# Latent attention written out over 64 query blocks, with projections by half tiles between them

## What is computed

```python
q = jnp.einsum("bsr,re->bse", rmsnorm(c_q, q_norm_g[l]), w_q_up[l])
q = q.reshape(b, s, MLA_HEADS, MLA_QK_DIM)            # 64 plain + 32 rotated
q_nope, q_rope = q[..., :MLA_NOPE_DIM], q[..., MLA_NOPE_DIM:]
q_rope = apply_rope(q_rope, cos, sin)
kv = jnp.einsum("bsr,re->bse", rmsnorm(c_kv, kv_norm_g[l]), w_kv_up[l])
k_nope, v_mla = kv[..., :MLA_NOPE_DIM], kv[..., MLA_NOPE_DIM:]
k_full = jnp.concatenate([k_nope, broadcast(apply_rope(k_rope, cos, sin))], -1)
o_mla = chunk_causal_softmax_attention(q_full, k_full, v_mla)
```

## Time and profile before

| | |
|---|---|
| median of 3 runs | 3533.0 us (3526.06 to 3537.19) |
| profiled execution | 3531.41 us, of which the span of its instructions 3529.6 us |
| `latent_attention` in it | first matmul at 688.16 us, last VectorE instruction starts at 1067.61 us |
| busy over the span | PE 3006.8 (85%), DVE 1612.5 (46%), ACT 1256.4 (36%), POOL 711.3 (20%) |

### The profile page before, as it was taken

How to read it: one execution, slowest core, us unless ns; L and a number is a source line. 1 busy time by engine, 2 the same in 40 slices (tenths; PEclk the granted TensorE clock), 3 DMA queues, 4 the chain that set the end, 5 groups by cost and what they waited for, 6 DMA issues and landing times. The chain is left out here.

```text
span 3529.6 us, 35907 instructions
## 1 busy us (share of the span) xinstructions
PE 3006.8 (85%) x13416; PEld 2422.7 (69%) x13416; DVE 1612.5 (46%) x1983; ACT 1256.4 (36%) x2003; POOL 711.3 (20%) x317
## 2 busy tenths in 40 slices
PE   6999998766668859989889899977686998998998
PEld 5787886555556747767767677754475787787786
DVE  3665651356654333777877787511432221111121
ACT  3555541344442143555555445432223111111110
POOL 2111111100002211323332233211312121121211
PEclk8999999888869979999999999988798999999999
DMA  4111222000004312121221112133230111111112
GB/s 111 38 54 48 66 67 59 18 8 7 9 0 146 111 66 63 48 61 38 62 60 50 55 51 75 69 137 107 95 125 18 48 48 42 42 48 42 42 48 72
DMA packets 232494, 207.77 MB, mean 59 GB/s; under 512 B 25224, under 2 KB 196776, under 8 KB 232360
## 3 DMA queue, kind: packets, MB, share of 16 engines
q1 hardware_dynamic: 231328, 204.40, 18.6%
q10 hardware_dynamic: 1032, 1.57, 0.3%
HBM read 156.13 MB, written 41.42 MB: 56 GB/s over the span
## 5 line engine op out<-in xcount | busy, mean ns | idle before, releaser
L179 POOL TENSOR_TENSOR w_lo<-w_raw,w_hi 128x1024 fp32r<-128x1024 f32 (+2 forms) x228 | 536.5, 2355 | 2214.7 <-ACT w_hi L171 2214.7
L171 ACT ACTIVATE w_hi<-w_raw 128x1024 fp32r<-128x1024 f32 (+2 forms) x228 | 223.7, 985 | 780.1 <-PE u_y_ps L1649 222.4
L2272 DVE SCALAR_TENSOR_TENSOR d_acc<-d_padded,vectors,d_acc 128x1024 f32<-128x1024 f32 x240 | 397.2, 1655 | 4.5
L197 PE MATMUL d_pp<-h_hi,w_hi 128*128 128x512 f32 x896 | 368.0, 411 | 12.2 <-PEq L67 5.2
L197 PE MATMUL d_pp<-h_hi,w_lo 128*128 128x512 f32 x896 | 368.8, 412 | 0.0
L197 PE MATMUL d_pp<-h_lo,w_hi 128*128 128x512 f32 x896 | 366.0, 408 | 0.0
L197 PE MATMUL s_pp<-h_hi,w_hi 128*128 128x512 f32 x512 | 206.8, 404 | 12.1 <-PEq L67 12.1
L197 PEld LDWEIGHTS d_pp<-h_hi,w_hi 128*128 128x128 f32 x896 | 175.1, 195 | 56.0 <-issue 18.0
L2056 POOL TENSOR_TENSOR d_probs<-d_probs 128x128 f32<-128x128 f32 (+3 forms) x64 | 123.5, 1930 | 410.4 <-ACT d_probs L2170 410.2
L197 PE MATMUL s_pp<-h_hi,w_lo 128*128 128x512 f32 x512 | 205.2, 401 | 0.0
L197 PE MATMUL s_pp<-h_lo,w_hi 128*128 128x512 f32 x512 | 204.2, 399 | 0.0
(11 more groups left out here) (320 smaller groups left out, 6621.0 us busy)
## 6 DMA issues: line engine op xcount, KB each, us to landing
w_raw<-in_w_in SPq DMA_DIRECT2D x97, 512.0 KB, 4.0
w_raw<-in_w_gate_up SPq DMA_DIRECT2D x44, 512.0 KB, 3.9
w_raw<-in_w_down SPq DMA_DIRECT2D x22, 512.0 KB, 3.8
gates<-s_gate SPq DMA_DIRECT2D x16, 512.0 KB, 5.2
f_gate<-gates SPq DMA_DIRECT2D x16, 512.0 KB, 4.8
w_raw<-in_w_out SPq DMA_DIRECT2D x16, 512.0 KB, 4.1
w_raw<-in_w_proj SPq DMA_DIRECT2D x16, 512.0 KB, 5.0
x_tok_in<-in_x SPq DMA_DIRECT2D x8, 512.0 KB, 8.5
```

The source lines that it names most:

```text
L171: act.activation(self.hi[:, s, 0:chunks, :], self.raw[:, s, 0:chunks, :], ACT.Copy).then_inc(self.rounded[s], 1)
L179: pool.tensor_tensor(self.lo[:, s, 0:chunks, :], self.raw[:, s, 0:chunks, :], f32(self.hi[:, s, 0:chunks, :]), ALU.subtract).then_inc(self ...
L197: mm = pe.matmul(halves(ps)[h], w[:, k, :], x[:, k, h * HALF:(h + 1) * HALF], start=(k == 0 and r == 0), stop=(k == chunks - 1 and r == 2))
L2272: dve.scalar_tensor_tensor(out=acc[:, :], in0=x, scalar=wt, in1=acc[:, :], op0=ALU.mult, op1=ALU.add).then_inc(c["taps"], 1)
```

## The change

`latent_attention` is written anew, in the form of one sequence of 64 units (8 heads by 8 blocks) plus 4 steps that empty it, with no loop and no `convert` between pairs:

- **Projections.** There are 16 tiles in a list: `X` and `Y` (the rotated parts of four heads at a time, plain and with halves swapped), `N` (the 64 plain query rows of two heads), `K`, `V`. The first five are made before step 0, by halves of 512 tokens in the four halves of the score buffers. The others are made in 22 halves of 6 or 9 matmuls at the steps of the table `when`, each between the scores and the turning of that step, into one bank `pp`. ScalarE rounds a half straight from PSUM and VectorE subtracts straight from PSUM (`take`, `split`); `m_raw` is gone.
- **Copies.** Queries and keys are put in place by DMA, SBUF to SBUF: six transfers per head (two of 128 KB, four of 256 KB), on SP's queue between the weight loads.
- **Banks.** Both chunks of turned probabilities go into `bank[n % 2]`, never into the score buffers. The value tile is turned at step 6 of each head, for the next head, through the same two banks in two halves (64 turnings in all, before 32).
- **Turned probabilities** have two buffers `t_hi`, `t_lo`, and the values are multiplied four steps behind (before three), after the turning of that step.
- **VectorE order.** In a step, the norm of unit `s-1` stands ahead of the maximum of unit `s`. The maximum is negated in the same instruction; the scale is in the queries, so L1159 is gone. The gate is applied in 16 pieces of 64x512.
- `latents` loads the rotation table as two tiles of 128 rows, in 8 transfers instead of 1, and keeps its inverse roots in a part of the gate tile that is not written yet.
- The weights of the next stage are rounded at step 46.

```diff
-    PAIRS, UNITS, ROWS = SB_W // P, 2 * QB, 64
-    TILES = 4
+    UNITS, LAG = HEADS_ * QB, 4
+    STEPS = UNITS + LAG
...
+        when = {5: (-1, 1), 6: (2, 3), 7: (8, 9), 8: (18, 19), 9: (20, 21), 10: (22, 23), 11: (24, 25), 12: (26, 27),
+                13: (33, 34), 14: (36, 37), 15: (41, 42)}
...
+            def copy(head):
+                a, p = head % 2, head // 2
+                r = slice(head % 4 * ROPE, (head % 4 + 1) * ROPE)
+                if head >= 2:
+                    sp.wait_ge(c["scored"], QB * (head - 1))
+                sp.wait_ge(c["r_low"], head // 4 + 1)
+                for dst, src in ((q_hi, r_hi), (q_lo, r_lo)):
+                    sp.dma_start(f32(dst[NOPE:QK, a, :]), src[r, :].bitcast(F32)).then_inc(copied[a], 16)
...
+            after = {6: (0, 1), 9: (2, 3), 12: (4,), 13: (5,)}
@@ ScalarE @@
+            for s in range(STEPS):
+                head, at = s // QB + 1, s % QB
+                if s < UNITS:
+                    expose(s)
+                for t, h in halves_at(s):
+                    take(t, h)
+                if at == CONV_V and head < HEADS_:
+                    for x in range(2):
+                        round_v(head, x)
+                if 2 <= s < UNITS + 2:
+                    for x in range(CHUNKS[(s - 2) % QB]):
+                        round_t(s - 2, x)
+                if s >= LAG and (s - LAG) % 2 == 1:
+                    copy_low((s - LAG) // 2)
@@ VectorE @@
+            for s in range(STEPS):
+                head, at = s // QB + 1, s % QB
+                if 1 <= s <= UNITS:
+                    norm(s - 1)
+                if s < UNITS:
+                    top(s)
+                for t, h in halves_at(s):
+                    split(t, h)
...
+                if 2 <= s < UNITS + 2:
+                    for x in range(CHUNKS[(s - 2) % QB]):
+                        low_t(s - 2, x)
+                if s >= LAG and (s - LAG) % 2 == 1:
+                    add_low((s - LAG) // 2)
@@ TensorE @@
+            for s in range(STEPS):
+                head, at = s // QB + 1, s % QB
+                if s < UNITS:
+                    score(s)
+                for t, h in halves_at(s):
+                    fill(t, h)
+                if at == CONV_V and head < HEADS_:
+                    for x in range(2):
+                        turn_v(head, x)
+                if 2 <= s < UNITS + 2:
+                    for x in range(CHUNKS[(s - 2) % QB]):
+                        turn_t(s - 2, x)
+                if s >= LAG and (s - LAG) % 2 == 1:
+                    values(s - LAG)
```

More of the change, by code:

```diff
@@ L818, in latents @@
         square = mem.sb("l_square", [P, 2, TOK])
[L819 removed]
+        inv = [gate_silu[:, n, :] for n in (2, 3)]
         turn = square
@@ L975, in latent_attention @@
-        pp = mem.ps("m_pp")
+        o_sb = mem.sb("m_o_sb", [P, HALF])
+        pp = mem.ps("m_pp", [P, HALF])
         sc = [mem.ps(f"m_sc{i}") for i in range(2)]
[L977 to L985, removed]
@@ L1000, in latent_attention @@
[L1000 to L1004, removed]
-        complete = [next(u for u in range(UNITS) if runs[u][1] >= ENDS[j]) for j in range(TILES)]
-        first_chunk = [sum(CHUNKS[x % QB] for x in range(u)) for u in range(UNITS + 1)]
-        rows = [slice(0, ROWS), slice(ROWS, P)]
-        EACH = 2 * N_CHUNKS
-        def turned_into(u, c):
-            return sc[(u + 1) % 2][:, HALF:TOK] if c else bank
@@ L1014, in latent_attention @@
-        ring.phase(PAIRS, 3, 3, 2, 2, ahead=ahead)
+        bank = [mem.ps(f"m_bank{i}", [P, HALF]) for i in range(2)]
+        o_ps = mem.ps("m_o_ps", [P, 2 * P])
+        names = """n_round n_low k_round k_low taken_v turned_x turned_y r_sum r_round r_low scored masked maxed prob inverse
+            normed turned t_round t_low pv o_copied o_done gate_mul""".split()
+        c = {n: mem.sem(f"m_{n}") for n in names}
+        copied = [mem.sem(f"m_copied{i}") for i in range(2)]
+        COPIES = 6
@@ new lines, in latent_attention, with halves_at, bank_of @@
+        round_at = {7: 2, 8: 5, 9: 11, 10: 20, 11: 22, 12: 24, 13: 29, 14: 34, 15: 38}
+        AHEAD_AT = 46
+        def halves_at(s):
+            return [(t, h) for t in when for h in range(2) if when[t][h] == s]
+        banks = [half for x in sc for half in halves(x)]
+        def bank_of(t, h):
+            return banks[(2 * t + h) % 4] if t < EARLY else pp[:, :]
+        first = [N_CHUNKS * (u // QB) + sum(CHUNKS[:u % QB]) for u in range(UNITS + 1)]
+        CONV_V = 6
+        order = [("v", 0, 0), ("v", 0, 1)]
@@ L1015, in latent_attention @@
+        ring.phase(1, *(len(source(t)) for t in range(TILES)), ahead=ahead)
         block = stack.enter_context(nc.Block())
@@ new lines, in fill, with turn_v @@
+            def fill(t, h):
+                own(t, 3 * chunks[t] * h, 3 * chunks[t] * (h + 1))
+            def turn_v(head, x):
+                n = number["v", head, x]
+                pe.wait_ge(c["taken_v"], 2 * (head // 2 + 1))
+                if n >= 2:
+                    pe.wait_ge(c["t_low"], n - 1)
+                for b in range(4):
+                    t = pe.transpose(bank[n % 2][:, b * P:(b + 1) * P], v_raw[:, (4 * x + b) * P:(4 * x + b + 1) * P],
+                                     ident[:, :])
+                t.then_inc(c["turned"], 1)
@@ new lines, in values @@
+            def values(u):
+                g, (head, b) = u // 2, divmod(u, QB)
+                pe.wait_ge(c["t_low"], number["t", u, CHUNKS[b] - 1] + 1)
+                if g >= 1:
+                    pe.wait_ge(c["o_done"], g)
+                for k in range(b + 1):
+                    q0 = P if k == b else 0
+                    for x, t in enumerate((t_hi, t_lo)):
+                        mm = pe.matmul(o_ps[:, q0:2 * P], v2[:, k, head % 2].rearrange("p x d -> p (x d)"),
+                                       t[:, g % 2, k, q0:2 * P], start=(k == 0 and x == 0), stop=(k == b and x == 1))
+                mm.then_inc(c["pv"], 1)
```

537 lines of the change are left out of this document (276 added, 261 removed).

## The result

The changed kernel runs in 3484.0 us (median of 4 runs, 3477.4 to 3488.6) against 3535.1 of the kernel before (4 runs, 3526.1 to 3537.7): a ratio of 0.9859, with an interval of 0.9834 to 0.9883. The forecast was 3488 and 45 us less; 51 us less were measured. The profiled execution took 3477.4 us, its span is 3475.5.

The account below looks back on a forecast made before the run. No engine is full; a chain of hand-offs bounds the stage. First mask 717 plus 254 + 10 + 10.5 + 15.5 + 11 + 8 gives 1026, 45 us less: 3488 us, eight in ten from 3460 to 3515.

Parts of the forecast that it names:

- Step 7: Beginning of the stage, with five tiles and the copies for heads 0 and 1: first mask at 717, maybe 713 or 723.
- Step 1 and 2: Chain of eight heads at 31.8 us, 254 us, plus the gate's 16 multiplications on VectorE's path, 10 us.
- Step 3: Values' turning, seven times in the loop, with value halves first in both banks: 1.5 us each, 10.5 us.
- Step 4 and 5: Half tiles in the loop: ScalarE's and VectorE's work on them 15.5 us, TensorE late at them 11 us.
- 6, end: Steps 64 to 67, which empty the sequence: 8 us, then 0.85 us to the next stage.
- the 10 us a head: Kernel before, steps with two chunks: TensorE late by a taken score buffer or value matmuls ahead; expected to go.
- filled against unfilled pair: Kernel before: 91 us against 74, less 8 for `convert`, is 9 per pair or 27 for three.
- rival C: Slower: TensorE at 1.2 GHz throughout, decides if the mean clock falls below 0.52; 3551 us, chance 0.03.
- B: TensorE still ends the steps with many half tiles: 32 us more than A, 3520 us, chance 0.16.
- A: The forecast: the chain as summed, TensorE's lateness at half tiles between 0 and 25; 3470 to 3505 us, chance 0.60.
- The hidden case: Additions, gate and takes fall into unseen waits, up to 30 of 47 us go; 3458 us, chance 0.15.
- D: No change: the old waits return in another place, for instance score buffers; 3525 to 3540 us, chance 0.06.

Follow-up runs that it names:

- experiment 1: Changed kernel with VectorE's norm of unit s-1 behind the maximum of unit s: 3444.4 us, ratio 0.9746.
- Experiment 5: Changed kernel with the next head's value halves turned one each at steps 4 and 5, not both at step 6: 3467.0 us, ratio 0.9816.
- experiment 4: Changed kernel with only the first and last matmul of each half tile in the loop, so not the reference's values: 3477.9 us (1 run).
- experiment 3: Changed kernel with the half tiles of steps -1 and 1 at steps 2 and 3, the next two at 4 and 5: 3476.2 us (1 run).
- experiment 12: Changed kernel with values three steps behind, one buffer of turned probabilities, second piece in the score buffer, values ahead of the turning: 3524.2 us, ratio 0.9973.
- 11: Changed kernel with values three steps behind, one buffer of turned probabilities, and values ahead of the turning on TensorE: 3498.2 us, ratio 0.9896.
- experiment 10: Changed kernel with norm behind the maximum, value halves at steps 4 and 5, first half tiles at steps 2 to 5: 3428.9 us, ratio 0.9710.
- experiments 6 and 7: Each against the changed kernel. First: values three steps behind, one buffer of turned probabilities, 3515.4 us. Second: second piece in the score buffer, 3508.7 us.
- experiment 9: Changed kernel with values three steps behind, one buffer of turned probabilities, and the second piece in the score buffer: 3543.5 us, ratio 1.0036.
- the ladder: Kernels from the one before to the changed one, stages 383.9, 385.4, 356.1, 342.2, 340.5 us; the first step is a bundle, the others one edit each.

## Why the prediction was right, and where it only came out

The mechanism was right, the direction and the size too: 3484 against 3488, 43.4 us of stage against 45, and 306.4 us from the first mask to the next stage's first transfer where the text named 310. But the sum is better than its terms, and that it came within 2 us of the stage is luck: three terms missed by +5, +14 and -17 us and cancelled.

| step of the prediction | predicted, us | measured, us |
|---|---|---|
| 7, first matmul to first mask | 28.8 | 34.1 |
| 1 and 2, eight heads with the gate | 264 | 8 x 32.8 = 262 |
| 3, seven turnings of values | 10.5 | 7 x 3.5 = 24.5 |
| 4 and 5, half tiles | 26.5 | 9 |
| 6, end (measured: what is left) | 8.85 | 10.5 |
| stage | 339 | 340.5 |

The last line before the sum takes up what the others leave: the first head, which has no low parts or values to work on at first and holds the half tiles of steps 1 to 3, is counted like a full head without tiles.

*Step 1 and 2 held to one per cent,* and piece by piece. The last head has neither turning nor half tile and takes 32.8 us; the prediction had 31.8 + 1.3. In it VectorE is busy for 21.0 us (the prediction's terms for VectorE sum to 21.9) and idles 10.4 us under exponentials and roundings (predicted 10.0 and 1.1 for hand-offs). Only 1.1 us of its waits go back to TensorE (0.5 for scores, 0.6 for the copy of o), so the 10 us a head are gone as forecast. That the norm goes on the path was forecast and priced at 4.16 + 1.2, and experiment 1 took 4.6 us a head off by moving it. What I did not ask is whether the change needs it there. It doesn't: norm(s - 1) waits for the exponentials of the step before, and nothing in the new order of banks and buffers hangs on its standing first.

*Step 3 was mis-sized,* and beyond its upper bound of 2.5. Head 7, with a turning and no half tile, takes 36.3 us against 32.8 for the last. I had rounding 0.4, low part 0.42 and turning 0.6 plus hand-offs, as if one half were in the way. The row shows 2.10: VectorE's low parts follow the pair of roundings, the first four turnings of the probabilities take 1.1 us from issue to ScalarE's start, and both wait their turn. The scores behind it add 0.51. The last 0.9 of the 3.5 lies in other steps of the head (0.25 from block 7 to 0, 0.66 from block 1 to 2), and no run tells what it is. Experiment 5 shows the cause from the other side.

*Step 4 and 5 were too high by 17.* Heads 2 to 6, which hold 18 of the half tiles, take 36.7, 39.3, 40.9, 37.1 and 36.0 us against 36.3 with a turning alone: 9 in sum. TensorE's lateness, put at 11, is about 4 (experiment 4, at its lower clock). The waits of ScalarE and VectorE for `m_pp` in the loop sum to 3.6 us where I named 11. The comparison by which I sized them, filled against unfilled pair, had the old kernel's collisions of scores and low parts in it, and these are not a property of the tiles. It also priced 0.65 a half for ScalarE; 9 - 4 = 5 us over 18 halves is 0.3. Most of a rounding falls where ScalarE would wait anyway.

*Step 7 was 5.3 short,* though inside its bounds of 713 to 723, counted from the first matmul too (24.8 to 34.8; the stage began 3 us earlier). The prediction named the right wait, of ScalarE's half tile of step -1 for both heads' copies, and sized it too low: issuing the twelve takes from 702.42 to 713.66, 11.2 us and not about 6, and the last lands 5.3 us after its issue began and not 3 to 4. It also took the wait as given, where VectorE's order makes it one: experiment 3 moves the half tile and has 6.0 us back.

*The clock.* Granted was 0.80 over the stage (0.79 before), and the sum did not need it, but for the 2 us that it moved at the stage's end. The experiments bear on it more: the same 1200 matmuls, in stages of 385.4, 356.1, 340.5, 305.6 and 281.8 us, came with 0.75, 0.78, 0.80, 0.86 and 0.88 (windows of experiments 12 and 11, the changed kernel, 1 and 10). The shorter the chain around them, the nearer the mean to 2.4 GHz, in tendency: experiments 6 and 7 have stages of 368.3 and 367.2 us at 0.79 and 0.75, experiment 3 has 333.2 us at 0.79, so a stage's length alone doesn't give its clock. The tendency is the direction of the Trainium skill, "TensorE: Matmul & The Clock Gate", section "HAM oscillation — how this bites in real kernels", by which waits between bursts put the engine back to half rate. For rival C to decide, the mean would have had to fall under 0.52; the lowest seen in any of these stages is 0.75 (0.745 in experiment 9).

*The other rivals.* B (TensorE ends the steps) wanted 32 us more than A; all that the heads with half tiles cost is 9, and experiment 4 gives 4 of it to TensorE. The hidden case was half true: it was the half tiles that were hidden, and the turnings cost what they gave. D would have shown a head of over 36 us without half tiles or turning. The chances had a slip: A, B and the hidden case sum to 0.91, less than the 0.92 given to "faster".

*Where the gain came from* was ahead of me only in part. I had put the ten us a head down to the score buffer and the value matmuls alike. Of the 43.4 us the ladder gives two thirds (29.2) to the second piece's bank, a third (14.0) to the buffers with the fourth step, and next to nothing to the order; but with one buffer the order is worth 12 us, the other way round. The end of `convert` shows no gain of its own: it stands in the ladder's first step together with the norm's move, and the two aren't told apart.

## What to carry over

When a chain alternates between two engines, each work item that isn't on the chain belongs behind the instruction that hands over, under the other engine's turn; look for it in the time order of one step before counting anything else (here 35 us for two swapped calls). A buffer shared by two uses can cost what stands behind its user in the same queue: here a second user that took one of two banks at a time cost 0.3 us a head in its steps, and one that took both at once 2.1 to 2.6. And undo a part together with the order it was written for, or the experiment prices a kernel that never was.

## What was not expected of the hardware

TensorE's busy time isn't a property of its work. The same 1200 matmuls showed 262.8 us busy in the stage of experiment 12 and 220.4 in that of experiment 10, at 0.75 and 0.88 of the clock. Busy time of TensorE from a slow chain thus overstates what it would need in a shorter one. Whether that helped the three gains together to 2 us more than their sum isn't shown: it is within the scatter.

Twelve transfers within SBUF, one behind the other on SyncE's queue, were issued 0.6 to 1.4 us apart (702.42 to 712.44), and ScalarE, which waited for the last, went on 5.4 us after its issue began, where the 256 KB transfers of another stage landed in 3.1 us. Down the row the landing grew from 2.3 us for the first (128 KB) to 5.3 for the last (256 KB), while the core's 16 DMA engines were busy for 86% of the time from 702 to 713.5 and moved 189 GB/s.
